# Value products of a head pair as one group of 40, with six buffers of turned weights, in a hybrid layer stack on one core

## What is computed

```python
q = rotary(rms_norm(q, q_norm_g)); k = rotary(rms_norm(k, k_norm_g))      # 16 heads of 64, 4 key heads
s = einsum('bnqhgd,bnjhd->bhgnqj', qb, kwin) * HEAD_DIM ** -0.5           # blocks of 128, window of 3 blocks
s = where(abs(kpos - qpos) <= 128, s, -1e30)
m = maximum(max(s), sink)
p = exp(s - m); p = p / (sum(p) + exp(sink - m))
o = einsum('bhgnqj,bnjhd->bnqhgd', p, vwin)
return o * silu(gate)
```

## Time and profile before

| | |
|---|---|
| Median of 3 runs | 3005.22 us (3004.83 to 3005.74) |
| The profiled execution's own time | 3005.3 us |
| Its span, first to last instruction | 3003.5 us |
| Mean granted TensorE clock | 0.998 |
| PE busy | 2970.7 us (99%) |
| DVE, POOL, ACT busy | 1775.4 (59%), 1413.9 (47%), 1179.0 us (39%) |
| Attention steps t = 3 to 23 | 603.65 to 699.25 us in the first layer, 1599.09 to 1694.83 us in the second |

### The profile page before, as it was taken

One profiled execution on the slowest core, in us unless ns is written; L12 is line 12 of the kernel. 1 busy time (PEld: TensorE's weight loads), 2 busy tenths in 40 slices (PEclk: granted clock), 3 DMA queues, 4 the chain that ended last, 5 costly groups with the idle time before them and its releaser, 6 DMA issues.

```text
span 3003.5 us, 41965 instructions
## 1 busy us (share of the span) xinstructions
PE 2970.7 (99%) x14220; PEld 2435.8 (81%) x14220; DVE 1775.4 (59%) x2681; ACT 1179.0 (39%) x1771; POOL 1413.9 (47%) x1040
## 2 busy tenths in 40 slices
PE   8999999999999999999999999999999999999998
PEld 6888888877888888888887788878888888788886
DVE  7986577885525598568688744367773243611214
ACT  4233333474333424333346533246554323522223
POOL 5443443455555543443354555544344545454544
PEclk9999999999999999999999999999999999999999
DMA  4322222212233322222221232222222322233222
GB/s 151 98 72 76 91 84 78 85 43 99 91 98 101 126 91 85 84 86 75 78 91 50 78 101 96 97 91 69 73 82 85 112 85 98 92 98 98 92 97 91
DMA packets 73273, 267.91 MB, mean 89 GB/s; under 512 B 8128, under 2 KB 9024, under 8 KB 72768
## 3 DMA queue, kind: packets, MB, share of 16 engines
q1 hardware_dynamic: 70560, 254.84, 26.0%
q10 hardware_dynamic: 2592, 11.46, 1.0%
HBM read 262.07 MB, written 4.19 MB: 89 GB/s over the span
## 4 chain that ended last, share of the span: by engine, by line
PE 85%; issue 7%; POOL 5%; DVE 2%; ACT 0%; DVEq 0%; POOLq 0%; ACTq 0%
PE gem L384 19%; PE gem L386 19%; PE gem L385 19%; POOL wlo L317 5%; PE gem L787 2%; PE gem L789 2%; PE gem L788 2%; PE gem L505 2%; PE gem L506 2%; PE gem L507 2%; PE gem L625 2%; PE xp L687 1%; PE gem L627 1%; PE gem L626 1%; PE xp L671 1%
## 5 line engine op out<-in xcount | busy, mean ns | idle before, releaser
L317 POOL TENSOR_TENSOR wlo<-raw,whi 128x512 fp32r<-128x512 f32 x956 | 1317.1, 1399 | 1530.0 <-ACT whi L949 1530.0
L949 ACT ACTIVATE whi<-raw 128x1024 fp32r<-128x1024 f32 x478 | 504.5, 1056 | 675.1 <-PE gem L386 507.1
L384 PE MATMUL gem<-zhi,whi 128*128 128x512 f32 x1680 | 655.9, 390 | 0.3 <-DVE zlo L1593 0.3
L386 PE MATMUL gem<-zhi,wlo 128*128 128x512 f32 x1680 | 653.9, 389 | 0.0
L385 PE MATMUL gem<-zlo,whi 128*128 128x512 f32 x1680 | 653.6, 389 | 0.0
L384 PE MATMUL gem<-hhi,whi 128*128 128x512 f32 x1296 | 505.2, 390 | 0.0
L386 PE MATMUL gem<-hhi,wlo 128*128 128x512 f32 x1296 | 504.3, 389 | 0.0
L385 PE MATMUL gem<-hlo,whi 128*128 128x512 f32 x1296 | 504.2, 389 | 0.0
L384 PEld LDWEIGHTS gem<-zhi,whi 128*128 128x128 f32 x1680 | 315.4, 188 | 66.4 <-DVE zlo L1593 0.8
L386 PEld LDWEIGHTS gem<-zhi,wlo 128*128 128x128 f32 x1680 | 315.3, 188 | 66.0
L385 PEld LDWEIGHTS gem<-zlo,whi 128*128 128x128 f32 x1680 | 315.4, 188 | 65.5 <-issue 0.2
(11 more groups left out here) (418 smaller groups left out, 4329.6 us busy)
## 6 DMA issues: line engine op xcount, KB each, us to landing
raw<-in_slabs SPq DMA_DIRECT2D x478, 512.0 KB, 3.4
U<-in_x SPq DMA_DIRECT2D x4, 512.0 KB, 7.6
U<-in_x ACTq DMA_DIRECT2D x1, 2048.0 KB, 8.4
xsave<-U ACTq DMA_DIRECT2D x1, 2048.0 KB, 6.6
U<-xsave ACTq DMA_DIRECT2D x1, 2048.0 KB, 8.9
out_y<-yr SPq DMA_DIRECT2D x8, 256.0 KB, 2.2
tab<-in_tab_ret ACTq DMA_DIRECT2D x2, 512.0 KB, 7.9
tab<-in_tab_att ACTq DMA_DIRECT2D x2, 512.0 KB, 3.6
```

What stands on the lines that cost most here:

```text
L317: part = pool.tensor_tensor(wlo[:, k % 4, c], raw[:, k % 2, c], whi[:, k % 4, c].bitcast(f32), O.subtract)
L384: pe.matmul(o, wh, hi, start=(n == 0), stop=False)
L386: mm = pe.matmul(o, wl, hi, start=False, stop=(n == len(terms) - 1))
L949: act.activation(whi[:, k % 4, :], raw[:, k % 2, :], A.Copy).then_inc(hi_done, 1)
```

## The change

- `PT` gets three sets of two buffers, one for each step of a pair: in `U_C`, in the places that `ZT` had, and in `U_DT`. `ZT` goes.
- `a_pv(p)` now does all 40 value matmuls of a pair at once. It stands in step c = 0 of pair p + 2, right behind the scores and ahead of the turns; for p = 6 behind step 23, for p = 7 behind two gate slabs. It waits for all six turned buffers of its pair, and for p above 0 for `z_ready` of p splits, that is until `head_split(p - 1)` is done.
- `gated_head` writes its product back into bank 3 of `xp`, and `head_split` reads it from there. `ao_read` goes; `ao_done` counts pairs instead of steps.
- The full rows of steps 1 and 2 are cut so that each has one row behind the turns (step 2: two ahead, one behind, before three ahead).
- ACT's `turned_p(t)` waits for the values of the pair before its own.
- The last rotation is cut in two and moved: `turned(9)` to the end of step 9, `joined(9)` to the end of step 12. `turn_p(1)` no longer waits for it.
- After step 23 the second gate slab is cut by turns of 23: three rows, turns, five rows.

```diff
-        PT = [[U[:, a + n * T:a + (n + 1) * T] for n in (2, 3)] for a in (U_C, U_SG)]
+        PT = [[U[:, U_C + 2 * T:U_C + 3 * T], U[:, U_C + 3 * T:U_C + 4 * T]],
+              [U[:, U_VT + 3 * T:U_VT + 3 * T + 3 * P], U[:, U_VF + T:U_VF + T + 3 * P]],
+              [U[:, U_DT:U_DT + 3 * P], U[:, U_DT + 3 * P:U_DT + 6 * P]]]
...
-                def a_pv(t):
-
-                    p, c = t // 3, t % 3
+                def a_pv(p):
+
                     pr = p // 4
-                    if c == 0 and p:
-                        pe.wait_ge(ao_read, L * 8 + p)
-                    pe.wait_ge(t_ready, L * 48 + t * 2 + 2)
-                    for n, cols in spans(c):
...
+                    if p:
+                        pe.wait_ge(z_ready, L * 40 + 16 + p + PRIMED)
+                    pe.wait_ge(t_ready, L * 48 + p * 6 + 6)
+                    for c in range(3):
+                        for n, cols in spans(c):
...
-                    else:
-                        rows(4 + p, (0, 2, 5)[c], (0, 4, 8)[c])
+                    elif c:
+                        rows(4 + p, (0, 2, 5)[c], (0, 4, 7)[c])
+                    if c == 0 and p > 1:
+                        a_pv(p - 2)
                     if t >= 3:
                         turn_p(t - 3)
-                    if t >= 4:
-                        a_pv(t - 4)
                     if t > 1:
-                        rows(4 + p, (0, 4, 8)[c], (2, 5, 8)[c])
+                        rows(4 + p, (0, 4, 7)[c], (2, 5, 8)[c])
+                a_pv(6)
                 turn_p(21)
-                a_pv(20)
...
-                hslab(G, 0, u)
...
+                gate_rows(0, 0, 8)
                 turn_p(22)
-                a_pv(21)
-                hslab(G, 1, u)
+                gate_rows(1, 0, 3)
                 turn_p(23)
-                a_pv(22)
-                a_pv(23)
+                gate_rows(1, 3, 8)
+                a_pv(7)
                 zslab(G, 2, u, (z_ready, L * 40 + 16 + PRIMED))
...
-                    if t > 1:
-                        act.wait_ge(ao_done, L * 24 + t - 1)
+                    if t > 2:
+                        act.wait_ge(ao_done, L * 8 + t // 3)
...
-                    dve.wait_ge(ao_done, L * 24 + (3 * p + 3))
-                    dve.drain()
-                    stt(ZT[p % 2], xp[:, 3, :], 0.5, SG[:, p % 2, :], O.mult, O.mult).then_inc(ao_read, 1)
+                    dve.wait_ge(ao_done, L * 8 + (p + 1))
+                    dve.drain()
+                    stt(xp[:, 3, :], xp[:, 3, :], 0.5, SG[:, p % 2, :], O.mult, O.mult)
 
                 def head_split(p):
 
-                    split(zhi[:, p, :], zlo[:, p, :], ZT[p % 2], z_ready)
+                    dve.drain()
+                    split(zhi[:, p, :], zlo[:, p, :], xp[:, 3, :], z_ready)
...
-                a_rotated(9)
                 for t in range(2, 24):
...
+                    if t == 9:
+                        turned(9)
+                    if t == 12:
+                        joined(9)
```

More of the change, by code:

```diff
@@ L152, in build @@
               [U[:, U_T + 14 * P:U_T + 17 * P], U[:, U_T + 17 * P:U_T + 20 * P]]]
-        PT = [[U[:, a + n * T:a + (n + 1) * T] for n in (2, 3)] for a in (U_C, U_SG)]
+        PT = [[U[:, U_C + 2 * T:U_C + 3 * T], U[:, U_C + 3 * T:U_C + 4 * T]],
+              [U[:, U_VT + 3 * T:U_VT + 3 * T + 3 * P], U[:, U_VF + T:U_VF + T + 3 * P]],
+              [U[:, U_DT:U_DT + 3 * P], U[:, U_DT + 3 * P:U_DT + 6 * P]]]
         TH = U[:, U_VT + 2 * T:U_VT + 3 * T]
-        ZT = [U[:, U_VT + 3 * T:U_VT + 4 * T], U[:, U_VF + T:U_VF + 2 * T]]
         MG, XN = tiles(U_A, 8), tiles(U_C, 8)
@@ L251, in build @@
             "s_done", "m_ready", "p_exp", "r_ready", "p_ready0", "p_ready1"))
-        t_done, t_ready, ao_done, ao_read, th_ready = (sem(n) for n in (
-            "t_done", "t_ready", "ao_done", "ao_read", "th_ready"))
+        t_done, t_ready, ao_done, th_ready = (sem(n) for n in (
+            "t_done", "t_ready", "ao_done", "th_ready"))
         csum, cmean, cssq, cvar, crstd, cn, cs = (sem(n) for n in (
@@ L663, in turn_p @@
                         pe.wait_ge(a_rs, L * 10 + 10)
-                    elif t == 1:
-                        pe.wait_ge(a_rope, L * 10 + 10)
                     for hf in range(2):
@@ L672, in turn_p @@
                         mm.then_inc(t_done, 1)
-                def a_pv(t):
-                    p, c = t // 3, t % 3
+                def a_pv(p):
                     pr = p // 4
-                    if c == 0 and p:
-                        pe.wait_ge(ao_read, L * 8 + p)
-                    pe.wait_ge(t_ready, L * 48 + t * 2 + 2)
-                    for n, cols in spans(c):
[L682 to L689, removed]
+                    if p:
[3 more added lines that the diff above has]
+                        for n, cols in spans(c):
+                            lo, hi = max(n - 1, 0), min(n + 2, 4)
+                            for j in range(lo, hi):
+                                at = cols.start + (j - lo) * P
+                                for hf in range(2):
+                                    d = slice(hf * 64, hf * 64 + 64)
+                                    mm = pe.matmul(xp[d, 3, n * P:(n + 1) * P],
+                                                   VTA[:, j, pr * P + hf * 64:pr * P + hf * 64 + 64],
+                                                   PT[c][hf][:, at:at + P], start=(j == lo), stop=(j == hi - 1))
                     mm.then_inc(ao_done, 1)
@@ L705, in layer, with gate_rows @@
                         rows(4, 1, 5)
-                    else:
-                        rows(4 + p, (0, 2, 5)[c], (0, 4, 8)[c])
+                    elif c:
+                        rows(4 + p, (0, 2, 5)[c], (0, 4, 7)[c])
+                    if c == 0 and p > 1:
+                        a_pv(p - 2)
                     if t >= 3:
                         turn_p(t - 3)
-                    if t >= 4:
-                        a_pv(t - 4)
                     if t > 1:
-                        rows(4 + p, (0, 4, 8)[c], (2, 5, 8)[c])
+                        rows(4 + p, (0, 4, 7)[c], (2, 5, 8)[c])
+                a_pv(6)
                 turn_p(21)
-                a_pv(20)
                 G, u = g0 + ATT_OUT[0], u0 + ATT_OUT[1]
-                hslab(G, 0, u)
+                def gate_rows(k, a, b):
+                    for r in range(a, b):
+                        if r == 0:
+                            pe.wait_ge(lo_done, G * 4 + (k + 1))
+                            pe.wait_ge(evac[k], u + PRIMED)
+                        wh, wl = (w[:, k, r * P:(r + 1) * P] for w in (whi, wlo))
+                        pe.matmul(gem[:, k, :], wh, hhi[:, r, :], start=(r == 0), stop=False)
+                        pe.matmul(gem[:, k, :], wh, hlo[:, r, :], start=False, stop=False)
+                        mm = pe.matmul(gem[:, k, :], wl, hhi[:, r, :], start=False, stop=(r == NT - 1))
+                        if r == NT - 1:
+                            mm.then_inc(slab_done, 1)
+                gate_rows(0, 0, 8)
                 turn_p(22)
-                a_pv(21)
-                hslab(G, 1, u)
+                gate_rows(1, 0, 3)
                 turn_p(23)
-                a_pv(22)
-                a_pv(23)
+                gate_rows(1, 3, 8)
+                a_pv(7)
                 zslab(G, 2, u, (z_ready, L * 40 + 16 + PRIMED))
@@ L1241, in turned_p @@
                         act.wait_ge(t_done, L * 48 + t * 2 + hf + 1)
-                        act.activation(PT[t % 2][hf][:, 0:w], xp[:, hf, 0:w], A.Copy).then_inc(t_ready, 1)
+                        act.activation(PT[t % 3][hf][:, 0:w], xp[:, hf, 0:w], A.Copy).then_inc(t_ready, 1)
                 def exps(t):
@@ L1966, in a_normed, with turned @@
                     stt(x, x, vec[:, C_KG:C_KG + 1], RS, O.mult, O.mult).then_inc(a_kn, 1)
-                def a_rotated(n):
+                def turned(n):
                     x = NORMED[n]
@@ L1978, in a_rotated, with joined @@
                     dve.stream_shuffle(RT[2], x, PARTNER)
+                def joined(n):
+                    x = NORMED[n]
                     dve.drain()
@@ L1985, in a_rotated @@
                     tt(x, RT[1], RT[2], O.add).then_inc(a_rope, 1)
+                def a_rotated(n):
+                    turned(n)
+                    joined(n)
                 dve.wait_ge(tab_in, L * 32 + 32)
```

## The result

| | before | after |
|---|---|---|
| Median | 3005.42 us (4 runs) | 3036.49 us (4 runs, 3034.8 to 3037.62) |
| Ratio after to before | | 1.0103, 95% interval 1.0086 to 1.0121 |
| Profiled execution's own time, its span | 3005.3, 3003.5 us | 3036.28, 3034.5 us |
| Mean granted TensorE clock | 0.998 | 0.993 |

The change makes the kernel 31 us slower.

The account below looks back on a forecast made before the run. PE, busy 99% of the span, was taken as the bound. Per layer, -4.9 (switches) - 0.3 (rotation) + 12.0 + 3.4 (waits) = +10.2 us; two layers +20.4 on 3005.3 gave 3026 us, range 3012 to 3036.

Parts of the forecast that it names:

- The gain without waits: Attention stage on PE: fewer changes of group save 0.68 us a pair, so 13.66 becomes 12.98 us.
- the switches: Changes of group on PE in the attention stage: fewer of them were to give -4.9 us a layer.
- the rotation: Last rotation leaves DVE's queue ahead of `maxes(2)`, shortening PE's wait behind the first turns: -0.3 us a layer (0 to -0.8).
- Scores to values: PE's switch from scores straight to values, not in the trace: taken as scores to turns, 0.90 including about 0.15 of switch.
- The wait: PE's values wait for DVE's split of the previous pair: 2.4 us for each of `a_pv` 1 to 5 per layer.
- the two behind step 23: Wait of `a_pv(6)`, once a layer with no scores between: 3.4 us (2.7 to 3.9).
- the split is late by its whole chain: Main forecast for DVE's step 2: split done 6.95 us after its scores, wanted at 4.56; 3026 us, chance 0.58.
- the second case: POOL's slab shifts out of DVE's small operations; tanh, gate and split alone set 1.9 us a wait; 3020 us, chance 0.18.
- The PSUM-reading cast at 0.69 us: Cast in DVE's split, now reading bank 3: 0.69 us in place of 0.42.
- `a_pv(7)`: Last values group of a layer: 33 full products and two turns ahead of it for its split, so no wait.
- the wait of `a_pv(6)` is the nearest to it: Wait behind step 23, likened to the 4.91 us wait with clock 0.50 behind it: +3.4 us once a layer.
- a rival with 0.14: Granted clock falls to 0.50 behind `a_pv(6)`'s wait: 3029 us, with the longest waits 3036; chance 0.14.

Follow-up runs that it names:

- split first: Changed kernel with the split of a pair's head moved from the end of step 2 to its start on DVE, ahead of the maxima: 2996.12 us.
- the kernel with the split in the middle: Changed kernel with the head's split moved between the maxima of step 2 and its reciprocals and gate: 3014.89 us.
- the filled kernel: Changed kernel with full-array products that nobody reads (8 or 12) on PE ahead of waits for the split: 3022.87 us.

## Why the prediction was right about the wait and wrong about the clock

**The gain without waits: right.** 12.98 us a pair was forecast and measured. Over the kernel, split first against before gives -9.3 us; with the 1.2 us of ACT waits taken out -10.5, against -9.8 for the switches and -0.6 for the rotation. The rotation's term is right as a wait (0.49 in place of some 0.8 us a layer), but it buys no time: put back ahead of the loop, it left the kernel as quick (2996.31 us).

**Scores to values: right.** 0.20 us from the last scores to the values; the price of a switch was there. The values next to the scores saved only the switch that fell away. As the Trainium skill has it (TensorEngine Tiling (Array Packing), Key Properties), a change of tiling mode drains the array. The trace agrees so far as the change costs time: 0.20 us from scores to values, where scores of this step start 0.11 apart.

**The wait: right in place and number, a little large.** Twelve places, as forecast. Between the last scores and the values lie 2.34 us in place of 0.20, so the wait costs 2.14 (forecast 2.4), and the two behind step 23 cost 3.2 (forecast 3.4): 10 x 2.14 + 2 x 3.15 = 27.7 us in place of 30.8. The step that was off is the forecast's own chain, "the split is late by its whole chain". PE's wait shifted POOL's slab onto the end of DVE's column operations, and tanh, gate and split set the time. That is the second case, which had 0.18, and it gives 1.9 a wait; the measured 2.14 lie between it and the forecast. That the forecast came within 0.3 us a wait is in part luck. The PSUM-reading cast at 0.69 us was right. `a_pv(7)` had 48 full products and three turns ahead of it, not 33 and two; it had no wait, as forecast. The Trainium skill (SBUF — State Buffer, two separate sides) has the two engines' shared ports held for whole instructions. The trace agrees: in the kernel with the split in the middle the second held operation ends at 644.98 us and POOL's second instruction at 644.95.

**The clock: this is the step that failed.** The forecast's sum held nothing for it. I wrote that "the wait of `a_pv(6)` is the nearest to it", and charged the clock once a layer, as a rival with 0.14. The row I had was a wait of 4.91 us; the next shorter one, at 17.65 us, was 1.21 us and had no fall behind it. Between them nothing was known, and the ten waits of 2.4 us lay between them, but I put them on the harmless side without a reason and had no bound for it. Measured, nine of twelve waits had 3.3 us at 0.50 behind them, and the filled kernel prices them at 13.6 us. Of the two longest, at which I had looked, one brought no fall.

**Sum:** -10.5 + 27.7 + 13.6 = +30.8 us, measured +31.1. The first two terms alone give 3022.6 us, and the filled kernel measured 3022.87. Without the clock the time would have been 3022.9 (the filled kernel), 3 us below the forecast.

## What to carry to other kernels

When a buffer is read back in place of a copy, the next writer waits for the last reader; look up on the reader's queue when that is, and what stands ahead of it only by habit. Here one DVE step moved to the head of its queue's step made the whole change a gain, **2996.12 us**, the fastest version found, 0.32% under before. And on a PE that is otherwise full, an idle stretch has two prices, its length and the clock behind it: work that nobody reads, put into the wait, tells the two apart, and gets the second one back.

## What the runs showed of the hardware

In the attention stages, where PE is otherwise full, idle stretches of 0.75 to 1.7 us left the granted clock at 1.00 in all 21 places where they stood; behind stretches of 2.06 us and more it fell to 0.50 in nine of twelve places in one kernel and in two of three in another. It was not the longest that decided: in the changed kernel one of 2.96 us had no fall behind it, and eight of ten of 2.06 had. Which ones are spared stays open; no run here took that apart.

Nor is 1.7 us a safe length everywhere. At the start of the program, where PE has worked only since some 11 us, the profiles of five of the kernels have a wait of 1.35 to 1.50 us with a stretch at 0.50 close behind it, and in the seven others the same wait was 0.82 to 1.27 us and had none. The filled kernel is one of the five:

```profile
17.44 0.50 PE L466 MATMUL gem<-zhi,whi 128*128 128x512 f32 x1 [1.35 <-DVE zlo L1704]
```

```profile
18.80:22.10 3.30, 3.30 (x9) 2.52 (x9) 2.96 (x5) 2.20 (x3) 0.72 (x1) 0.50 0.49 159
```

The idle time of 4.91 us that rows 9 show has one low stretch in some profiles and two on end in others. In the changed kernel both windows are at 0.50, and the first begins 2.7 us before the wait ends (2046.67):

```profile
2043.95:2047.30 3.35, 0.63 (x2) 0.54 (x3) 3.26 (x5) 2.57 (x5) 0.00 (x0) 0.50 0.00 0
2047.40:2050.70 3.30, 3.30 (x10) 2.56 (x9) 3.21 (x6) 3.17 (x5) 2.38 (x2) 0.50 0.00 0
```

In the kernel with the split first, the stretch begins 0.5 us before the wait ends, and the window behind it is back at 1.00. Both kinds of stretch come and go between profiles of kernels that do not differ there, and the kernel before measured at most 3006.33 us in its runs with a mean clock of 0.998 and at least 3006.47 in those with 0.997. This is one source of the 1 to 2 us by which runs of one kernel differ, and it is why differences of about 1 us between the quicker kernels above are not told apart.
